# Moving one head's sums and their copy within the unit loop of a recurrent mixer

## The reference

```python
def step(state, inp):
    r_t, w_t, k_t, v_t, a_t, b_t = inp
    sa = jnp.einsum('dbhij,dbhj->dbhi', state, a_t)
    state = (state * w_t[..., None, :] + sa[..., :, None] * b_t[..., None, :]
             + v_t[..., :, None] * k_t[..., None, :])
    y_t = jnp.einsum('dbhij,dbhj->dbhi', state, r_t)
    return state, y_t
```

## Time and profile before

| | us |
|---|---|
| median of 3 runs | 3745.22 (3741.4 to 3746.01) |
| profiled execution, its time | 3744.75 |
| profiled execution, its span | 3743.0 |
| TensorE busy in the span | 3479.2 (93%) |
| VectorE busy | 2335.3 (62%) |
| ScalarE busy | 1409.3 (38%) |
| mean granted TensorE clock | 0.975 |
| unit stage | about 1423 to 2188 us of the span |

### The profile page before, as it was taken

One profiled execution on the slowest core, in us unless ns is written; L12 is line 12 of the kernel. 1 busy time (PEld: TensorE's weight loads), 2 busy tenths in 40 slices (PEclk: granted clock), 3 DMA queues, 4 the chain that ended last, 5 costly groups with the idle time before them and its releaser, 6 DMA issues. The chain is left out here.

```text
span 3743.0 us, 56377 instructions
## 1 busy us (share of the span) xinstructions
PE 3479.2 (93%) x21081; PEld 2281.9 (61%) x21081; DVE 2335.3 (62%) x4283; ACT 1409.3 (38%) x2572; POOL 382.0 (10%) x679
## 2 busy tenths in 40 slices
PE   7999998799999997999999986899999959999998
PEld 5788886344444446777777773566777634444444
DVE  3555555799999944566665655777777734444443
ACT  3445444132332322222222204566666622323322
POOL 0343333000000002222222200000000000000000
PEclk9999999899999998999999998999999979999999
DMA  4353435522222224433333352300000041222121
GB/s 145 134 163 116 138 120 174 184 73 102 100 101 92 84 87 131 132 116 106 107 107 107 107 164 79 96 11 14 11 14 11 12 185 54 80 80 80 59 74 44
DMA packets 307944, 355.04 MB, mean 95 GB/s; under 512 B 122380, under 2 KB 234712, under 8 KB 305312
## 3 DMA queue, kind: packets, MB, share of 16 engines
q1 hardware_dynamic: 294304, 341.82, 27.8%
q10 hardware_dynamic: 13440, 10.49, 0.9%
HBM read 194.95 MB, written 157.29 MB: 94 GB/s over the span
## 5 line engine op out<-in xcount | busy, mean ns | idle before, releaser
L595 PE MATMUL cv_pj<-cv_uT,w 128*128 128x257 f32 (+1 forms) x2240 | 503.3, 382 | 0.0
L595 PEld LDWEIGHTS cv_pj<-cv_uT,w 128*128 128x128 f32 (+1 forms) x2240 | 410.4, 186 | 89.1 <-issue 21.8
L1592 PE MATMUL at_g<-at_kT,at_qz 64*128 64x512 f32 x1088 | 303.6, 634 | 30.8 <-DMA at_kT<-scratch_q_kT 25.5
L875 DVE TENSOR_TENSOR rs_tt<-rs_tt,rs_tmp 128x63 f32<-128x63 f32 (+31 forms) x315 | 288.9, 917 | 10.8
L873 DVE TENSOR_TENSOR rs_tmp<-rs_tt,rs_al 128x63 f32<-128x63 f32 (+31 forms) x315 | 284.2, 902 | 15.6 <-DMA rs_al<-scratch_ablk 6.0
L1615 PEld LDWEIGHTS at_pb<-at_v,at_attT 128*128 128x128 f32 x2176 | 249.8, 192 | 64.6 <-issue 47.0
L1544 DVE CUSTOM_DVE_ANT_0 at_sca<-at_g,at_nd 128x1024 f32<-128x1024 f32 (+1 forms) x144 | 167.8, 1166 | 183.5 <-PE at_g L1592 183.0
L1863 PE MATMUL fn_gb<-fn_wg,fn_hT 128*128 128x512 f32 x640 | 278.0, 592 | 1.7 <-ACT fn_hT L1722 1.7
L1863 PE MATMUL fn_hb<-fn_wo,fn_mixT 128*128 128x512 f32 x640 | 279.4, 594 | 0.3 <-ACT fn_mixT L1722 0.3
L1615 PE MATMUL at_pb<-at_v,at_attT 128*128 128x128 f32 x2176 | 265.1, 279 | 13.0 <-ACT at_attT L1502 13.0
L944 PE MATMUL rs_tm<-w,x_pair 128*128 128x512 f32 x480 | 214.1, 604 | 32.4 <-DMA rs_gains<-in_da_k_norm_dram 19.8
(11 more groups left out here) (256 smaller groups left out, 5773.7 us busy)
## 6 DMA issues: line engine op xcount, KB each, us to landing
un_pk<-scratch_packs SPq DMA_DIRECT2D x80, 640.0 KB, 3.9
scratch_packs<-cv_pk SPq DMA_DIRECT2D x19, 2048.0 KB, 6.7
w<-in_w_in_dram SPq DMA_DIRECT2D x6, 2048.0 KB, 12.0
x_pair<-in_x_dram SPq DMA_DIRECT2D x20, 512.0 KB, 3.6
scratch_uT<-cv_uT SPq DMA_DIRECT2D x5, 2048.0 KB, 7.9
scratch_ablk<-cv_ab SPq DMA_DIRECT2D x80, 128.0 KB, 3.6
rs_al<-scratch_ablk SPq DMA_DIRECT2D x5, 2048.0 KB, 8.9
scratch_gate<-rs_tok_out SPq DMA_DIRECT2D x40, 256.0 KB, 2.4
```

Of the source, the lines that this page charges most:

```text
L595: last = nc.tensor.matmul(pj[n % 3][0:r, 0:HALF], w[:, c, m * P:m * P + r], uT[b % 2][:, c, HALF * hf:HALF * hf + HALF], start=(c == 0), s ...
L875: last = nc.vector.tensor_tensor(target, target, part, ALU.add)
L1592: last = nc.tensor.matmul(gb[m][:, c * 512:(c + 1) * 512], qz[par][rows, h, :], kT[rows, h, at:at + 512], start=True, stop=True)
```

## The change

Each of the two streams gets a helper for one head's part: `sums(n, par, h)` on VectorE and `own(n, par, h)` on ScalarE.

- VectorE no longer starts a body with the first masks of m. The first masks of n + 2 stand at the end of body n, directly behind head 0's sums of n; unit 1's stand ahead of the loop. Head 1's sums of n - 1 are done in body n, behind the second masks of m and ahead of the wait for the local store and of the bonus products.
- ScalarE copies head 1's own part of unit n - 1 in body n, behind the copies of the transposes and ahead of the copy of the applied product.
- In the last body, both heads are finished there.

The streams of TensorE, GpSimd and SP are unchanged, and so are the semaphores and the counts that they wait for.

```diff
@@ ScalarE
                 if more:
                     turned(*nxt(n, j, par))
+                if n:
+                    own(n - 1, 1 - par, 1)
                 act.wait_ge(s["wz_ready"], n + 1)
...
                     nc.scalar.copy(local_out[par][ys, 0, :], ob[h][ys, 0:P]).then_inc(s["y_evac"], 1)
-                    act.wait_ge(s["carry_evac"], n * 4 + 2 * h + 10)
-                    nc.scalar.copy(carry_at(n, par, hs, slice(0, 2), 192, 256), ob[h][hs, 384:512].rearrange("p (d c) -> p d c", d=2)).then_inc(s["own_evac"], 1)
+                    if h == 0:
+                        own(n, par, 0)
+                if not more:
+                    own(n, par, 1)
+
+            def own(n, par, h):
+                hs = slice(64 * h, 64 * h + 64)
+                act.wait_ge(s["carry_evac"], n * 4 + 2 * h + 10)
+                nc.scalar.copy(carry_at(n, par, hs, slice(0, 2), 192, 256), ob[h][hs, 384:512].rearrange("p (d c) -> p d c", d=2)).then_inc(s["own_evac"], 1)
@@ VectorE
                 m, jm, pm = nxt(n, j, par)
-                if more:
-                    masked(m, pm, 0)
                 dve.wait_ge(s["q_ready"], n + 1)
...
                 if more:
                     masked(m, pm, 1)
+                if n:
+                    sums(n - 1, 1 - par, 1)
+                if more:
                     dve.wait_ge(s[f"local{pm}"], jm * 16 + 16)
                     products(m, pm)
                 dve.wait_ge(s["ad_ready"], n * 4 + 4)
                 if n < NCH:
                     dve.wait_ge(s[f"carry{par}"], j * 16 + 16)
-                for h in range(2):
-                    dve.wait_ge(s["out_ready"], n * 2 + h + 1)
...
+                sums(n, par, 0)
+                if n + 2 < NI:
+                    masked(n + 2, par, 0)
+                if not more:
+                    sums(n, par, 1)
+
+            def sums(n, par, h):
+                dve.wait_ge(s["out_ready"], n * 2 + h + 1)
+                hs, ys = slice(64 * h, 64 * h + 64), slice(64 - 64 * h, 128 - 64 * h)
+                for d in range(2):
+                    nc.vector.scalar_tensor_tensor(carry_at(n, par, hs, d, 0, 192), ob[h][hs, 192 * d:192 * d + 192], fp[par][hs, d:d + 1], ad[par][hs, d, :],
+                                                   ALU.mult, ALU.add).then_inc(s["carry_evac"], 1)
+                dve.wait_ge(s["y_evac"], n * 2 + h + 1)
+                nc.vector.tensor_tensor(local_out[par][ys, 0, :], ob[h][ys, 192:192 + P], local_out[par][ys, 0, :], ALU.add).then_inc(s["sum_evac"], 1)
...
             products(0, 0)
+            masked(1, 1, 0)
             chunks(dve, body)
```

## The result

The changed kernel takes 3750.0 us (median of 20 runs), the kernel before 3744.56 (20 runs, the first three among them). The ratio is 1.0014, 95% interval 1.0007 to 1.002: about 5 us slower, less than the 0.2% that the prediction called no change, and outside its range on the slow side. The profiled execution has a span of 3750.9.

A forecast was written before the change was run, and what follows sets the result against it. TensorE was taken as the bound, at 9.41 us a unit. 78 x 0.41 = 32.0 us saved less 78 x 0.26 = 20.3 given back made 11.7 less: 3733 us, range 3719 to 3747.

The forecast's parts named there:

- First masks earlier: VectorE's first masks start behind head 0's sums, so TensorE's second scores start sooner: 0.41 us a unit saved.
- Head 1's sums, ScalarE's copy, the new wait: Head 1's sums and copy delay the copy of the applied product; TensorE's outputs wait: 0.26 us a unit given back.
- S: Start of TensorE's second scores in a unit, from which the prediction counts the later starts, in us.
- The store and its queue: Bonus products wait for the local store just issued; landings of 1.7, or 2.0 in the first 20 units, cost nothing.
- Rival C: Local store collides with the load behind it, takes 2.9, first masks come late: 35 us on top, 3768; chance 0.07.

The follow-up runs named there:

- experiment 7: Changed kernel with three buffers for the local result and the heads' roles swapped, so head 0's sums and copy are put off: 3708.01 us, ratio 0.9909.
- experiment 6: Changed kernel, but SP holds each load back until the local store of unit n - 1 has landed: 3750.51 us, ratio 1.0018.
- experiment 1: Changed kernel with three buffers for the local result instead of two, so bonus products wait for the store of three units before: 3725.05 us, ratio 0.9953.
- experiment 5: Changed kernel with 96 semaphore instructions more on TensorE's stream, once, ahead of the unit loop: 3762.93 us, ratio 1.005.
- experiment 4: Kernel before with only the next first masks moved between the heads' sums; head 1's sums and copy stay in their unit: 3735.29 us, ratio 0.998.

## Why the prediction was wrong

*First masks earlier, 0.41 a unit:* right, except behind a late store. Joined product to second scores is 0.38 for the forecast 0.39, and VectorE waits 0.27 for line 1201 ahead of the first masks, as said.

*Head 1's sums, ScalarE's copy, the new wait, 0.26 a unit:* right, with every link. Masks at S + 1.05 (forecast 1.06), sums at S + 2.24 (2.24), head 1's copy at S + 3.04 (3.02), the copy of the applied product at S + 3.32 (3.31), outputs at S + 3.96 (3.94). The wait is 17.3 us in the trace for a forecast of 20.3; by the starts it is 0.28 a unit (3.96 - 3.68). The unit is 9.26 to 9.27 for a forecast of 9.26. That both engines are held by the change of partitions was argued from rows of before; experiment 7 shows it.

*The step that failed* is in "The store and its queue": "60 units hide the landing entirely ... Nothing is charged." The landing went in with its typical 1.7 and 2.0. In its new place one store in five takes 3.2 to 4.0 us. The prediction had a landing cost something from 2.55, and 2.2 in the first 20 units; the trace gives 2.67 and 2.32 (the landing less what the unit lasts beyond 9.27). So the late stores make 18.0 us of new waits, which outweigh the 11.8 (29.1 - 17.3) that the order had won.

Rival C had the place and the wait right, and the threshold to 0.1. It had the cause wrong, the load (experiment 6), and the form: all units a little, where 17 are hit, most of them by 1 us or more. Its 0.07 was too little because the only spread looked at, up to 2.6, was that of a store at another point of the unit, where a fetch of TensorE's instructions hardly ever followed it.

*The ends of the loop* were left out of the sum. They gave 3.8 us at the end, 2.4 of it by the granted clock, which the change may have had no part in.

Without the failed step the forecast stands: experiment 1, which only takes that wait away, has 3725 for a forecast of 3733. Of the 8 us left over, 3 to 4 are the last unit's and some 3 the clock at the start of the stage in the two traces, which no term of the sum had; the rest is within the interval of the ratio (12 to 23 us under the kernel before; forecast 11.7).

What stays open: why the last nine packets of a late store go out one by one once the fetch is through, and why a few fetches that start later than 1.4 us still meet packets that have not gone (in experiment 6 one at 1.85). No run told that apart.

## What to carry to other kernels

When a change puts a wait close behind a store, cost it by the slowest landings that the new place can see and not by the median, or give it another buffer: 1 KB a partition turned this change from slightly slower into 0.5% faster. A spread read at the old place says nothing of the new one. Before an instruction is put ahead of one that feeds the bounding engine, count all of its chain: here one copy on ScalarE, needed by nobody soon, gave back two thirds of what a unit had gained (9.41 to 9.27 instead of 8.98), though it could as well have stood behind. Where two halves of the partitions are worked one after the other, choose for the critical chain the half on which its neighbours start.

## What the runs showed of the hardware

- A store of 128 KB that lands in 1.7 us takes 3.2 to 4.0 when a 16 KB packet of TensorE's instructions is fetched while its packets go out, in the changed kernel from 1.0 to 1.6 us behind its issue. A sixteenth of the store's packets then starts 1.2 us late (experiment 6).
- TensorE's instructions were fetched in one such packet per 256 records of its stream, 1.26 units, and adding 96 instructions ahead of the loop moved the fetches by 0.47 of a unit (experiment 5).
- ScalarE, and not VectorE alone, starts an instruction only behind the end of the last one when it begins on other partitions: 0.28 from start to start of a 0.26 us copy, against 0.16 (experiment 7).
- 96 semaphore increments in a row on TensorE's stream start 0.15 us apart, but for one gap of 2.5 us, 17 us in all (experiment 5).
- At the end of the stage the granted clock in the last outputs was 0.61 to 0.63 before and 1.00 after the change. The wait of TensorE ahead of them (1.9 and 1.0 us) does not decide it: with 1.9 us it stayed at 1.00 in experiment 4.
